# Scaling the attention probabilities on GpSimd instead of ScalarE, in a two-block model on one core

## The reference

```python
def blocked_gqa(q, k, v):
    ...
    def one_block(qi):
        s = jnp.einsum("bqgrd,bkgd->bgrqk", qi, k)
        p = jax.nn.softmax(s, axis=-1)
        return jnp.einsum("bgrqk,bkgd->bqgrd", p, v)
```

## Time and profile before

| | us |
|---|---|
| median of three runs | 2702.45 (2702.32 to 2702.6) |
| the profiled execution | 2703.51 |
| its span in the trace | 2701.7 |
| PE busy | 2670.5 (99% of the span) |
| DVE busy | 1522.4 (56%) |
| ACT busy | 1169.4 (43%) |
| POOL busy | 26.7 (1%) |

### The profile page before, as it was taken

The page is one execution under the profiler, slowest core; times in us unless marked ns, Lnnn a source line. Parts: engine busy times, 40 slices in busy tenths (PEclk is TensorE's granted clock), DMA queues, the critical chain, the costliest instruction groups (busy, mean ns, idle before and its releaser), DMA issues.

```text
span 2701.7 us, 33823 instructions
## 1 busy us (share of the span) xinstructions
PE 2670.5 (99%) x13860; PEld 2196.2 (81%) x13860; DVE 1522.4 (56%) x2132; ACT 1169.4 (43%) x1722; POOL 26.7 (1%) x45
## 2 busy tenths in 40 slices
PE   9989999999989999999999999999999999999998
PEld 8777888888777888888888888887777888888887
DVE  7885444346885444344444356788977755544433
ACT  6784322225784322233222233455589353422221
POOL 0000000000000000000000000000000000000000
PEclk9999999999999999999999999999999999999999
DMA  6303333224303333223322342222223423333322
GB/s 216 94 2 110 101 94 97 96 84 146 93 2 110 101 95 98 96 96 95 100 94 96 99 137 86 77 72 70 77 86 96 133 88 100 96 100 94 98 94 67
DMA packets 75801, 255.55 MB, mean 95 GB/s; under 512 B 9088, under 2 KB 12288, under 8 KB 75264
## 3 DMA queue, kind: packets, MB, share of 16 engines
q1 hardware_dynamic: 73136, 240.29, 28.3%
q0 software_dynamic: 2512, 13.11, 1.3%
HBM read 241.30 MB, written 8.39 MB: 92 GB/s over the span
## 4 chain that ended last, share of the span: by engine, by line
PE 95%; DVE 3%; ACT 1%; issue 0%; DMA 0%; SPq 0%; DVEq 0%; ACTq 0%
PE PS L1453 28%; PE PS L1455 28%; PE PS L1454 28%; PE PS L1670 1%; PE PS L1412 1%; PE PS L1652 1%; PE PS L1473 1%; PE PS L1471 1%; PE PS L1472 1%; PE PS L1716 1%; PE PS L1490 0%; PE PS L1616 0%; PE PS L1492 0%; PE PS L1494 0%; DVE XBC L2269 0%
## 5 line engine op out<-in xcount | busy, mean ns | idle before, releaser
L1453 PE MATMUL PS<-HHI,WHI 128*128 128x512 f32 x2256 | 896.9, 398 | 0.0
L1455 PE MATMUL PS<-HHI,WLO 128*128 128x512 f32 x2256 | 878.9, 390 | 0.0
L1454 PE MATMUL PS<-HLO,WHI 128*128 128x512 f32 x2256 | 878.4, 389 | 0.0
L2157 DVE TENSOR_TENSOR WLO<-WR,WHI 128x1024 fp32r<-128x1024 f32 (+2 forms) x450 | 534.8, 1191 | 492.5 <-ACT WHI L1755 489.5
L1755 ACT CAST WHI<-WR 128x1024 fp32r<-128x1024 f32 (+2 forms) x450 | 458.1, 1019 | 445.9 <-PE PS L1455 424.5
L1453 PEld LDWEIGHTS PS<-HHI,WHI 128*128 128x128 f32 x2256 | 423.6, 188 | 94.1 <-issue 6.7
L1454 PEld LDWEIGHTS PS<-HLO,WHI 128*128 128x128 f32 x2256 | 423.7, 188 | 90.7 <-issue 6.0
L1455 PEld LDWEIGHTS PS<-HHI,WLO 128*128 128x128 f32 x2256 | 423.4, 188 | 89.2
L1454 PE MATMUL PS<-FLO,WHI 128*128 128x512 f32 x682 | 265.3, 389 | 0.0
L1455 PE MATMUL PS<-FHI,WLO 128*128 128x512 f32 x682 | 265.3, 389 | 0.0
L1453 PE MATMUL PS<-FHI,WHI 128*128 128x512 f32 x682 | 265.3, 389 | 0.0
(11 more groups left out here) (358 smaller groups left out, 2718.8 us busy)
## 6 DMA issues: line engine op xcount, KB each, us to landing
WR<-in_stream SPq DMA_DIRECT2D x402, 512.0 KB, 3.5
WR<-in_stream SPq DMA_DIRECT2D x32, 384.0 KB, 3.0
xkeep<-X POOLq DMA_DIRECT2D x3, 2048.0 KB, 8.5
X<-xkeep POOLq DMA_DIRECT2D x24, 256.0 KB, 5.4
WR<-in_stream SPq DMA_DIRECT2D x16, 328.0 KB, 3.9
ROT<-RQ SPq DMA_DIRECT2D x40, 64.0 KB, 2.0
X<-in_xin SPq DMA_DIRECT2D x8, 256.0 KB, 5.1
out<-X SPq DMA_DIRECT2D x8, 256.0 KB, 2.2
```

The lines of the kernel that those rows point to most:

```text
L1453: e.matmul(out, hi[:, i, :], xhi, start=first, stop=False)
L1454: e.matmul(out, hi[:, i, :], xlo, start=False, stop=False)
L1455: t = e.matmul(out, lo[:, i, :], xhi, start=False, stop=final)
L2157: e.tensor_tensor(lo, raw, hi.bitcast(F32), ALU.subtract).then_inc(S["dve_low"], 1)
```

## The change

The step `prs` leaves ACT and goes to POOL, as a tensor_scalar product with the same operands (the tile times RIN, in place). Its semaphore is now raised by POOL, and the transposes wait for that one. The numbers of the planner are all new: `TIMES` (among them `prs`, now an entry of POOL), `DELAY`, `HANDOVER`, `AHEAD` and `RESCALED`. With them every engine's order is another in places. The number of instructions of each kind is the same, but for the 64 that move and one load of an activation table fewer on ACT.

```diff
-RESCALED = ({(5, 3): 0, (6, 0): 2, (6, 1): 4, (7, 3): 6}, {(3, 2): 0, (5, 1): 2, (6, 0): 4, (7, 3): 6})
+RESCALED = ({(5, 3): 0, (6, 0): 2, (7, 1): 4, (7, 3): 6}, {(2, 1): 0, (5, 1): 2, (5, 3): 4, (7, 3): 6})
...
-    "prs": (("act", 0.86353),), "yv": (("act", 0.37204), ("dve", 0.46663),), "hv": (("dve", 0.54408),),
...
+    "nrm": (("dve", 0.2),), "prs": (("pool", 1.4392),), "yv": (("act", 0.37204), ("dve", 0.46663),), "hv": (("dve", 0.49199),),
...
-DELAY = {"v": 0.29785, "zsilu": 1.0528, "pace1": 0.47233, "pace2": 6.0781, "turned": 0.40256, "ss": 0.60265,
+DELAY = {"v": 0.069744, "zsilu": 1.0528, "pace1": 0.20014, "pace2": 5.3917, "turned": 1.4432, "ss": 0.65888,
...
-HANDOVER = 0.17528
+HANDOVER = 0.09319
...
             elif kind == "pT":
                 l, i = a
-                q.wait_ge(S["act_prs"], n["prs", l, i])
+                q.wait_ge(S["pool_prs"], n["prs", l, i])
...
-            elif kind == "prs":
-                l, i = a
-                k = i % 8
-                q.wait_ge(S["dve_nrm"], n["nrm", l, i // 2])
-                e.activation(PRS[PR_OF[i]], PRS[PR_OF[i]], ACT.Copy, scale=RIN[:, k:k + 1]).then_inc(S["act_prs"], 1)
...
+            elif kind == "prs":
+                l, i = a
+                k = i % 8
+                q.wait_ge(S["dve_nrm"], n["nrm", l, i // 2])
+                e.tensor_scalar(PRS[PR_OF[i]], PRS[PR_OF[i]], RIN[:, k:k + 1], None, ALU.mult).then_inc(S["pool_prs"], 1)
```

More of the change, by code:

```diff
@@ L159 @@
[L159 to L163, removed]
@@ L169 @@
-    "dt": (("act", 0.72013), ("dve", 1.0752),), "rcs": (("dve", 1.5),), "rope": (("dve", 1.1929),), "xtd": (("dve", 1.4718),),
-    "dta": (("dve", 0.3), ("act", 0.5), ("dve", 0.2), ("act", 0.3), ("dve", 1),), "dte": (("dve", 0.65517),),
-    "xd": (("dve", 0.7),), "stadd": (("dve", 0.88987),), "mask": (("dve", 0.91608),), "xc": (("dve", 1.2646),),
-    "w": (("dve", 0.7),), "ya": (("pool", 0.8231),), "goff": (("dve", 1.5),), "gyb": (("dve", 2.0358),),
-    "zout": (("dve", 0.49643),), "yz": (("act", 0.41163), ("dve", 0.88542),), "max": (("dve", 0.7),), "nrm": (("dve", 0.2),),
@@ new lines @@
+    "ytc": (("act", 0.62279),), "yb": (("pe", 0.45),), "qk": (("pe", 0.92),), "qhi": (("act", 1.164),), "qlo": (("dve", 1.3),),
+    "pT": (("pe", 0.45),), "pv": (("pe", 0.95),), "lp": (("pe", 0.80337),), "near": (("pe", 0.54816),),
+    "far": (("pe", 2.4533),), "ro": (("pe", 1.6172),), "romm": (("pe", 0.85906),), "gates": (("pe", 1.6395),),
+    "mean": (("pe", 0.34258),), "cmm": (("pe", 0.75796),), "macc": (("dve", 0.29525),), "cacc": (("dve", 1.1467),),
+    "high": (("act", 1.0031),), "uhi": (("act", 0.71),), "hhi": (("act", 0.64116),), "sq": (("act", 0.97064),),
@@ new lines @@
+    "root": (("act", 2.1826),), "silu": (("act", 1.8115),), "fhi": (("act", 0.27302),), "zsilu": (("act", 0.95),),
+    "conv0": (("act", 0.5476),), "xsilu": (("act", 0.4826),), "raw": (("act", 0.61),), "v": (("act", 1),),
+    "rsq": (("act", 0.61727),), "rroot": (("act", 1.35),), "xta": (("act", 0.51191),), "bt": (("act", 0.2954),),
+    "ex": (("act", 0.41767),), "dexp": (("act", 0.65),), "gsq": (("act", 1.4923),), "exp": (("act", 0.75),),
+    "pta": (("act", 0.6),), "fk": (("act", 3.087),), "qsilu": (("act", 1.2953),), "ca": (("act", 0.58175),),
@@ new lines @@
+    "scale": (("dve", 1.192),), "hlo": (("dve", 0.25557),), "acc": (("dve", 0.40327),), "gs": (("dve", 0.6781),),
+    "mul": (("dve", 0.54896),), "flo": (("dve", 0.16448),), "add": (("dve", 3.1397),), "xscale": (("dve", 0.62551),),
+    "conv": (("dve", 3.2),), "dt": (("act", 0.56356), ("dve", 0.86894),), "rcs": (("dve", 1.5),), "rope": (("dve", 1.1929),),
+    "xtd": (("dve", 1.5379),), "dta": (("dve", 0.3), ("act", 0.5), ("dve", 0.2), ("act", 0.3), ("dve", 1),),
+    "dte": (("dve", 0.36553),), "xd": (("dve", 0.7),), "stadd": (("dve", 0.88987),), "mask": (("dve", 1.3796),),
@@ new lines @@
+    "xc": (("dve", 1.2646),), "w": (("dve", 0.7),), "ya": (("pool", 0.79973),), "goff": (("dve", 1.5),),
+    "gyb": (("dve", 2.3622),), "zout": (("dve", 0.65879),), "yz": (("act", 0.42106), ("dve", 1.0087),), "max": (("dve", 0.7),),
+    "nrm": (("dve", 0.2),), "prs": (("pool", 1.4392),), "yv": (("act", 0.37204), ("dve", 0.46663),), "hv": (("dve", 0.49199),),
+    "cu": (("dve", 0.71489),), "rf": (("dve", 1.1253),), "tots": (("dve", 2.1297),), "up": (("dve", 0.75),),
+    "pick": (("dve", 0.42291),), "spread": (("act", 0.67708),), "half": (("act", 0.94384),), "ry": (("dve", 1.5185),),
@@ L185 @@
+DELAY = {"v": 0.069744, "zsilu": 1.0528, "pace1": 0.20014, "pace2": 5.3917, "turned": 1.4432, "ss": 0.65888,
+         "hsum": 0.10436, "picked": 0.11763, "lru": 3.6094, "sq": 0.81618, "third": 0.13953, "merged": 0.057832, "until": 0.15438}
 MAIN_BANKS = (5, 6, 7)
-HANDOVER = 0.17528
+HANDOVER = 0.09319
 LOG_EXP = "natural_log_exp_and_others"
```

32 lines of the change are left out of this document (12 added, 20 removed), and 12 rows, old and new, of the table TIMES.

## The result

The changed kernel takes 2707.84 us (median of 16 runs, 2706.29 to 2710.01), the kernel before beside it 2702.43 (16 runs). The ratio is 1.002, with a 95% interval of 1.0014 to 1.0027: 5.4 us slower where 6.8 us faster was forecast. The time lies inside the range, on the wrong side of the kernel before.

The account below looks back on a forecast made before the run. PE was taken as the bound, busy 2670.5 of 2701.7 us, so only its idle time could shrink. Terms -12.2 + 4.4 + 1.5 - 0.5 = -6.8 us gave 2695.7 us, with a range of 2689 to 2708.

Parts of the forecast that it names:

- -12.2, the waits behind ACT: Block 1's tails: of 13.9 us of PE waits laid on ACT, 12.2 us would go once scalings leave ACT.
- +4.4, what the new order takes back: Both layers: PE needs copied results sooner, five places at 0.7 us and three at 0.3 us, 4.4 us lost.
- POOL at 0.65 us: Each scaling on POOL was assumed to take 0.65 us, between bounds of 0.53 and 0.78, no longer than on ACT.
- The slow rival: Tails: a POOL scaling of 1.3 us holds up DVE, which takes ACT's place; 2708.5 us, up to 2712; chance 0.18.
- Nothing for `ya` in POOL's queue: POOL's queue in the tails: `ya` could delay scalings behind it; counted as nothing, bounds up to 4 us.
- +1.5 for the lock with DVE: Tails: POOL and DVE contend in SBUF, 3.0 us of DVE a tail; a quarter of 6.0 us reaches PE.
- -0.5 for the clock: Layer 1: fewer gaps might avoid PE's slow clock stretch; half of the 0.99 us at stake counted as gain.
- The last rival: ACT had not caused the waits, so relieving it does nothing; time as in the even case, about 2701 us; no separate chance.

Follow-up runs that it names:

- e2_order: The changed kernel's order with all scalings back on ACT instead of POOL: 2713.29 us, ratio 1.004 to the kernel before.
- e14_eighth: Changed kernel with layer 0's reciprocal of pair 4 moved up, `ya` early on POOL, and only 64 of 512 columns scaled: 2700.41 us (0.9993).
- e13_half_both: Changed kernel with layer 0's reciprocal of pair 4 moved up, `ya` early on POOL, and only 256 of 512 columns scaled: 2701.17 us (0.9997).
- e10_ya_nrm: Changed kernel with `ya` early in POOL's queue and layer 0's reciprocal of pair 4 moved up, all columns scaled: 2707.97 us (1.0023).
- e16_pick30: Kernel before, in its order, every second scaling on POOL except head-chunks 7 and 31, plus 30; `ya` early, the last behind head-chunk 27: 2701.50 us (0.9997).
- e4_nrm: Changed kernel with only layer 0's reciprocal of pair 4 moved up on DVE, right behind the exponential it needs: 2705.98 us (1.0014).
- e5_half: Changed kernel with POOL scaling only the first 256 of 512 columns, the rest left unscaled, no other step moved: 2702.82 us (1.0001).
- e9_ya: Changed kernel with only its eight `ya` products taken earlier in POOL's queue: 2706.85 us (1.0017).

## Why the prediction was wrong

Medians lead from one kernel to the other in four steps (the kernel before stood at 2702.2 beside the middle runs, so up to 0.2 us of a step is that difference):

| step | us | to |
|---|---|---|
| kernel before | | 2702.4 |
| the new order alone (e2_order) | +10.9 | 2713.3 |
| scalings off ACT, 0.44 us on POOL, two places repaired (e14_eighth) | -12.9 | 2700.4 |
| scaling 0.92 us (e13_half_both) | +0.8 | 2701.2 |
| scaling 1.57 us (e10_ya_nrm; the changed kernel is at 2707.8) | +6.8 | 2708.0 |

**-12.2, the waits behind ACT.** This step failed in its mechanism. The named waits (YLO, STF, STB, those of L1567 and L1575 for ACT PR) did go, but they are gone in e2_order too, with all scalings on ACT, so the order removed them and not the relief. In the old order the relief of 6.9 and 6.5 us a tail (e16_pick30, where POOL has taken those scalings over) left most of them standing. STF and STB come back as waits of 0.68 and 0.60 us in e4_nrm, with no scaling on ACT. The 12.9 us of the table have nearly the forecast's size by luck: they are measured inside the new order, whose own waits for ACT (8.4 and 6.3 us in the first two rows of e2_order) the kernel before had not had, and they hold the two repairs as well.

**+4.4, what the new order takes back.** This step failed too: with the scaling left on ACT it is 10.9 us. The price of a place was right (0.7 us; in the changed kernel the three `pv` that were named waited 0.77, 0.82 and 0.77 and the two `yb` 0.69 and 0.68), but the count was not. I compared distances only for transposes with their own copy behind them. The list of e14_eighth names what I had left out: `dec` behind the copy that frees its bank (2 x 0.7), `dec` behind an exponential (1.0), the state-space products behind the last convolution (1.2), and more `pv`. The reciprocal of pair 4 stood in the same order on DVE, behind nine other instructions, and I had looked only at PE and ACT there. As each of these two terms depends on the other, only their sum can be judged: -7.8 us was forecast, and with the scaling at 0.44 us and both repairs it is -2.0. That is 5.8 of the 12.1 us of error.

**POOL at 0.65 us.** This step failed too, and with what hangs on it it is the larger part. From e14_eighth to the changed kernel it is 7.4 us (2700.41 to 2707.84), where the terms for DVE and the clock had 1.0 together: 6.4 us of the error. The 7.4 hold the late reciprocal and the late `ya` as well; the length alone, between 0.92 and 1.57 us, is worth 5.0 us without the repairs (e5_half) and 6.8 with them. The bounds of 0.53 and 0.78 were built on the thought that an operation reading one tile must be faster than one reading two. The slow rival went to 1.3, and the run shows 1.57. The row for the two-input product (1.04 us) was no upper bound. The diff itself held a warning which I read as one of the planner's numbers: its entry for `prs` on POOL is 1.4392 us, and on ACT 0.86353, where the trace had 0.742.

**Nothing for `ya` in POOL's queue.** Wrong in this form. I had looked for `ya` holding up scalings, counted nothing and left up to 4 us in the bounds. In the changed kernel scalings hold up `ya`: DVE waited 7.9 us for it over both layers. Moving `ya` ahead brings 1.0 us there and 6.0 in the order before. The mechanism I named exists too, and shows when `ya` comes early: in e10_ya_nrm PE waited 1.35 and 1.41 us for the scalings behind two of them.

**+1.5 for the lock with DVE.** The size of the load was right: 2.9 and 3.1 us of DVE a tail (64.04 against 61.15, and 66.49 against 63.43, in e2_order), with 3.0 forecast. It is luck in part, since the scaling was twice as long as assumed, and it cost an instruction of DVE some 0.4 us where the `ya` cost 0.85; and it cost POOL as much, for which the sum has no term. That a quarter of it reaches PE was not tested.

The Trainium skill's rule ("SBUF — State Buffer", "Who interferes with whom") fits the `ya`: the instruction of DVE that began at 774.04, with a `ya` running until 775.02, took 1.53 us in place of 0.68. It does not fit the scaling: of the two that began at 204.82 the second ended at 206.53, before the scaling did (206.86), so it had not waited for its end, and both had got longer. Its line that GpSimd is near line rate with one input ("GPSIMD Engine Reference", "Engine selection") does not hold here: 1.57 us for one input, 1.04 for two, and 0.92 for 256 columns where the one-input product Z of that size took VectorE 0.34 (two of them 0.60, overlapping).

**-0.5 for the clock.** Wrong in sign: layer 1 stayed at 0.98, and in layer 0 the clock fell to 0.50 behind a gap of 3.48 us. In the profiled execution it stayed there for ten microseconds, which costs 2.7 us of PE's busy time (65.07 against 62.39 in e4_nrm); in most executions it must be less, as the medians of the two kernels are only 1.9 us apart.

**The rivals.** The slow one gave 2708.5 us and the kernel takes 2707.8, but it is not what happened. It wanted DVE 90 to 95% busy, and DVE is at 83 and 87% (64.04 of 77.01 and 66.49 of 76.25). POOL's latency and queue stopped PE, not DVE's load. It did name the right switch, a scaling beyond 1.1 us. The chances stood at 0.50 for faster on a duration that no row showed, and with bounds that each came from another operation. The last rival, that ACT had not been the cause, was put aside by the list of waits; for the waits named there, e2_order and e16_pick30 speak for it.

What stays open: why the median of e10_ya_nrm is 2.0 us over that of e4_nrm when the two traces differ by 0.5, what the relief of ACT is worth apart from the order, since no run takes all scalings off ACT in the old order without putting them on POOL, and whether an order planned with 1.57 us and with the hand-overs as measured would beat 2701.5.

## What to carry to other kernels

Before work moves to an engine, find the duration of that very operation there. A row of another operation with more inputs is no upper bound, and if there is no such row, the range must show it. A wait that a list puts down to an engine need not go when that engine is relieved: try the order alone, without the move, before crediting the move. Waits of one hand-over stay, and a tighter order makes more of them, so count these on every engine for each result that PE asks for, the small steps such as a reciprocal among them. Where a queue gets a new long step, ask both ways: what does it hold up, and what holds it up.

## What was not expected of the hardware

- The one-input product with a scalar per partition, 128 rows in float32, took 442 ns for 64 columns, 922 for 256 and 1567 for 512 on POOL. That is about 0.28 us and 2.5 ns a column ((1567 - 442) / 448). The two-input product took 1.04 us for 512 columns.
- Both sides pay when the scaling meets an instruction of DVE with two inputs in SBUF. Beside the scaling at 204.76, which took 2.10 us in place of 1.57, two such instructions took 1.71 in place of 1.28; in e10_ya_nrm one scaling took 2.00 us. With two inputs on POOL it is DVE that loses more (2.13 in place of 1.28, the `ya` 1.26 in place of 1.04).
- Gaps of PE and what the granted clock did behind them don't go together simply. A gap of 3.48 us was followed by ten microseconds at 1.2 GHz in the changed kernel, and one of 3.50 us by a mean of 0.66 over five microseconds and 1.00 after that in e9_ya. Five gaps of 0.5 to 1.2 us within ten microseconds were followed by no fall in e4_nrm (mean clock of that tail 1.00), but two of 0.71 and 1.02 us were in e14_eighth (0.67 from 195 to 200 us). In the kernel before, one of 1.69 us in layer 1 was followed by the fall of the earlier trace rows, and its twin of 1.67 us in layer 0 by none (mean clock of that tail 1.00).
